# Three attentions of a two-layer block: scores ahead of values, side work behind the next step's maxima

## The chip, the cores and the metric

One core of a Trainium2 chip runs the whole kernel. The metric is the device time of one execution in microseconds (us); before the change the median of three runs is 1392.32 us (1392.32 to 1393.35).

## The reference, cut to what matters

256 tokens of width 1024 pass through two blocks. The first has an attention and a gated mixer, then a mixture of 16 experts (each 1024 to 2048 to 1024, top choices by capacity). The second has a layer with two attentions (causal, and sliding window with sinks), then a layer with a causal attention whose scores carry a cumulative forget gate. The core of all attentions is the same:

```python
s = jnp.einsum('bqhd,bkhd->bhqk', qi, k) * scale      # + bias, gate or window
s = jnp.where(mask, s, -jnp.inf)
p = jax.nn.softmax(s, axis=-1)
out = jnp.einsum('bhqk,bkhd->bqhd', p.astype(v.dtype), v)
...
return x + (o * jax.nn.silu(gate)) @ w_out
```

## The kernel before, in words

Each engine has its own program, written out by hand, and they meet in semaphores: `pe_program`, `dve_program`, `act_program`, `pool_program`, `sp_program`. An engine works strictly in the order of its program. TensorE (PE) multiplies, VectorE (DVE) and ScalarE (ACT) work on SBUF and PSUM, GpSimd (POOL) does a few small things and subtractions, SP issues the loads.

Weights come through a ring of seven slots of 2 MB. SP goes through the list of loads in order (L754 to L757); before each it waits until the slot's former content has been used. Three loads go to places lent by other tiles; two of them wait for the last values of the first attention (L290). Where accuracy wants it a weight is split in two: ACT rounds a quarter of it (`hi_piece`, L448, its instruction L454), then DVE or POOL subtracts (`lo_piece`, L456, L460).

PSUM has eight banks. `banks.take` deals six of them (`ALL6`) in turn; whoever takes one waits until its former content is out. Two banks are kept for the attentions' outputs.

An attention is a row of steps, each with two halves (g or r = 0, 1) of 512 scores per token. A step n has this chain:
- scores: PE (first attention L898; second L1136, L1139; third L1212, L1214);
- maxima: DVE (L1450, L1451; `largest`, L596 to L607, which also copies the scores to SBUF);
- exponents: ACT (L1936; `exponents`, L615, L618);
- division: DVE (L1460, L1462; `divide`, L625 to L630);
- transposes: PE (L479);
- copy of the transposed probabilities to SBUF: half 0 on ACT, half 1 on DVE (`probabilities_out`, `turned_out`; instructions L510 and L508);
- values: PE (L915, for two steps at a time; `values_flipped`, L582).

The first attention has 8 steps (`A1`), the second and third have 6 each (`A2`, `A3`), first one with 128 keys, two and two with 256, one with 128.

In iteration n PE does scores n, a turn, transposes n-1, a turn, values n-1. DVE does the end of a gate (`gate_finish`), maxima n, a turn, the gated product of an output that ended, copy n-1, division n, a turn, the gated low part. ACT does exponents n, copy n-1, the gated high part, and two turns (in the first attention one turn stands before the copy).

A turn runs one piece of side work from a generator. In the first attention (`beside`) that is, on PE: modulation products `mod_part` (L777), the spatial mixing (L839), columns (`mod_cols`, L789) and parts of the out-projection (L502); on DVE and ACT: its mixtures, weight splits and modulation rows. In the second and third attention it is the gate's projection: PE does it in quarters (`gate_matmuls`, L681); after each fourth quarter DVE multiplies (L716), ACT takes tanh (L699), and DVE finishes with `gate_finish` (L729) in the next iteration. ACT also splits weights (`gate_act`): the first four pieces go to POOL, the rest to DVE after the attention. When an output has ended, `gated` makes the product (DVE, L655), the high part (ACT, L663) and the low part (DVE, L659), which waits for the high part. Then come the out-projections (L502 second, L490 third attention).

```python
    def turn(side):
        next(side, None)
```

Of the kernel before, what the change touches and what calls it, by code (L numbers as in the profile page):

```python
# [139 lines left out]
def body(ctx, nc, A, kin, out):  # L140
# [620 lines left out]
    def pe_program(pe):  # L761
# [100 lines left out]
        def beside():  # L862
# [21 lines left out]
            for n2 in (1, 2):  # L884
                out_part(n2, True)
                yield

        side = beside()
        for n in range(9):
            if n < 8:  # L890
                i, hn = A1[n]
                for g in range(2):
                    banks.take((1, "s", n, g), ALL6)
                for g in range(2):
                    pe.wait_ge(banks.was[1, "s", n, g])
                pe.wait_ge(out_of(("QT", 0)), out_of(("QT", 1)), out_of("KT"))
                for g in range(2):
                    pe.e.matmul(PS[:, banks.of[1, "s", n, g], :], QT[64 * g:64 * g + 64, i, 128 * hn:128 * hn + 128],  # L898
                                KT[64 * g:64 * g + 64, :], start=True, stop=True).then_inc(*pe.mark((1, "s", n, g)))
            turn(side)  # L900
            if n:
                for g in range(2):
                    pe.wait_ge((1, "p", n - 1, g))
                    transposes(pe, (1, "t", n - 1, g), ALL6,
                               [PB[(2 * (n - 1) + g) % 4][:, 128 * s:128 * s + 128] for s in range(4)])
            turn(side)
            if n and n % 2 == 0:
                batch, i = n // 2 - 1, (n - 1) // 4
                if batch % 2 == 0:
                    banks.take((1, "o", i), (OB[i],))  # L910
                    pe.wait_ge(banks.was[1, "o", i])
                pe.wait_ge(out_of(("kv", 3)), *[out_of((1, "t", m_, g)) for m_ in (n - 2, n - 1) for g in range(2)])
                for s in range(4):
                    for g in range(2):
                        m = pe.e.matmul(PS[64 * g:64 * g + 64, OB[i], 256 * (batch % 2):256 * (batch % 2) + 256],  # L915
                                        KV[:, s, 128 + 64 * g:192 + 64 * g], PTB[batch % 2][:, s, g, :], start=s == 0,
                                        stop=s == 3)
                m.then_inc(*pe.mark((1, "pv", batch), *([(1, "o", i)] if batch % 2 else [])))
        rest(side)

# [200 lines left out]
        for n in range(len(A2) + 1):  # L1121
            if n < len(A2):
# [9 lines left out]
                for hh in range(len(step["heads"][0])):  # L1132
                    for r in range(2):
# [7 lines left out]
                        score_mark(pe, m, "e", n, r, hh == len(step["heads"][0]) - 1)  # L1141
            turn(side)
            if n:
                for r in range(2):
                    pe.wait_ge(("e", "p", n - 1, r))
                    transposes(pe, ("e", "t", n - 1, r), ALL6,
                               [A2_PB[(2 * (n - 1) + r) % 4][:, 128 * s:128 * s + 128] for s in range(4)])
            turn(side)
            if n:
# [4 lines left out]
                else:  # L1154
                    pe.wait_ge(out_of(("kvup", 1, 1)))
                    values_flipped(pe, "e", A2[n - 1], n - 1, A2_PT, 2, lambda s, h: VM[:, s, h, :])
        rest(side)

# [42 lines left out]
        pe.wait_ge(*[out_of((nm, n2)) for nm in ("q0", "q1", "k0", "k1") for n2 in range(2)], out_of("flT"), "kq")  # L1201
        for n in range(len(A3) + 1):
            if n < len(A3):
# [5 lines left out]
                for hh in range(len(step["heads"][0])):  # L1209
                    for r in range(2):  # L1210
# [5 lines left out]
                        score_mark(pe, m, "o", n, r, hh == len(step["heads"][0]) - 1)  # L1216
            turn(side)
            if n:
                for r in range(2):
                    pe.wait_ge(("o", "p", n - 1, r))  # L1220
                    transposes(pe, ("o", "t", n - 1, r), ALL6,
                               [A3_PB[(2 * (n - 1) + r) % 4][:, 128 * s:128 * s + 128] for s in range(4)])
            turn(side)
            if n:
                pe.wait_ge(*[out_of(("vf", h, i)) for h in range(2) for i in range(2)])
                values_flipped(pe, "o", A3[n - 1], n - 1, A3_PT, 2, lambda s, h: VF[:, s, 64 * h:64 * h + 64])
        rest(side)
        for i in (1, 0):
# [23 lines left out]
    def dve_program(dve):  # L1252
# [188 lines left out]

        side = beside()
        for n in range(9):
            if n < 8:
                i, hn = A1[n]
                for g in range(2):
                    idx = 8 * i + 4 * g + hn
                    c = slice(idx, idx + 1)
                    dve.wait_ge((1, "s", n, g))
                    dve.settle(dve.e.tensor_reduce(mx1[:, c], PS[:, banks.of[1, "s", n, g], :], AX.X, ALU.max))  # L1450
                    dve.e.tensor_scalar(nm1[:, c], mx1[:, c], -0.125, None, ALU.mult).then_inc(*dve.mark((1, "nm", n, g)))  # L1451
            turn(side)
            if n:
                probabilities_out(dve, n - 1, 1)
            if n < 8:
                for g in range(2):
                    idx = 8 * i + 4 * g + hn
# [3 lines left out]
                    p = PB[(2 * n + g) % 4]  # L1461
                    dve.e.tensor_scalar(p, p, sm1[:, c], None, ALU.mult).then_inc(*dve.mark((1, "p", n, g)))  # L1462
            turn(side)
            if n == 5:
# [196 lines left out]
        dve.wait_ge(*[out_of((name, hp)) for name in ("QMT", "KMT") for hp in range(4)], "bias")  # L1661
        for n in range(len(A2) + 1):
            gate_finish(dve, "e", late)
            if n < len(A2):
                step, nk = A2[n], A2[n]["nk"]
                for r in range(2):
# [7 lines left out]
            turn(side)  # L1674
            ended = A2[n - 2] if n >= 2 and A2[n - 2]["last"] else None
            if ended:
                gated(dve, None, "e", ended, OT, ("product",))
            if n:
                turned_out(dve, "e", n - 1, 1, A2_PT, 2)
            if n < len(A2):  # L1680
                for r in range(2):
                    divide(dve, "e", A2[n], n, r, A2_PB[(2 * n + r) % 4], sm2 if A2[n]["part"] == "mla" else sm3,
                           columns(A2[n], r, 8), sinks=A2[n]["part"] == "swa")
            turn(side)
            if ended:
# [93 lines left out]
        dve.wait_ge(out_of("cumulated"))  # L1779
        for n in range(len(A3) + 1):  # L1780
            gate_finish(dve, "o", late)
# [6 lines left out]
            turn(side)  # L1788
            ended = A3[n - 2] if n >= 2 and A3[n - 2]["last"] else None
            if ended:  # L1790
                gated(dve, None, "o", ended, OT3, ("product",))
            if n:
                turned_out(dve, "o", n - 1, 1, A3_PT, 2)
            if n < len(A3):
                for r in range(2):
                    divide(dve, "o", A3[n], n, r, A3_PB[(2 * n + r) % 4], sm4, columns(A3[n], r, 16))
            turn(side)
            if ended:
# [45 lines left out]
    def act_program(act):  # L1844
# [83 lines left out]
        act.wait_ge(out_of(("QT", 0)), out_of(("QT", 1)), out_of("KT"), "kr")  # L1928
        for n in range(9):
            if n < 8:  # L1930
                i, hn = A1[n]
                for g in range(2):
# [5 lines left out]
                        *act.mark((1, "e", n, g), out_of((1, "s", n, g))))  # L1938
            turn(side)
            if n:  # L1940
                probabilities_out(act, n - 1, 0)
            turn(side)
            if n == 5:
# [115 lines left out]
        for n in range(len(A2) + 1):  # L2059
            if n < len(A2):  # L2060
                swa = A2[n]["part"] == "swa"
                for r in range(2):
                    exponents(act, "e", A2[n], n, r, A2_PB[(2 * n + r) % 4], nm3 if swa else nm2, sm3 if swa else sm2,
                              columns(A2[n], r, 8), sinks=swa)
            if n:
                turned_out(act, "e", n - 1, 0, A2_PT, 2)
            if n >= 2 and A2[n - 2]["last"]:
                gated(None, act, "e", A2[n - 2], OT, ("high",))
# [36 lines left out]
        for _ in range(4):  # L2105
            turn(side)
        for n in range(len(A3) + 1):
            if n < len(A3):
                for r in range(2):
                    exponents(act, "o", A3[n], n, r, A3_PB[(2 * n + r) % 4], nm4, sm4, columns(A3[n], r, 16))  # L2110
            if n:
                turned_out(act, "o", n - 1, 0, A3_PT, 2)
            if n >= 2 and A3[n - 2]["last"]:
                gated(None, act, "o", A3[n - 2], OT3, ("high",))
# [201 lines left out]
```

## Time and profile before

| | us |
|---|---|
| median of three runs | 1392.32 |
| the profiled execution's own time | 1392.85 |
| its span | 1391.1 |
| TensorE busy | 993.2 |
| VectorE busy | 408.8 |
| ScalarE busy | 239.8 |
| GpSimd busy | 81.8 |
| share of DMA in the chain that ended last | 57% |
| share of TensorE in that chain | 32% |

The span is what the profile covers; the execution's own time has 1.75 us more around it. Busy times are sums over the span and say nothing of what lies beside what. "Idle before" with a releaser is the time that an engine stood idle before an instruction, and whose end released it. Times within the span are counted from its start.

### The profile page before, as it was taken

The page shows a single profiled execution, that of the slowest core. Times are in us where ns is not written, and L with a number is a line of the kernel's source. Part 1 is how long each engine was busy: PE and PEld are TensorE (multiplying, and loading weights), DVE is VectorE, ACT ScalarE, POOL GpSimd, SP SyncE. Part 2 cuts the span into 40 slices and gives each one's busy share as a digit, 9 for nine tenths or more (in the row PEclk, how much of TensorE's full clock was granted, in tenths as well). Part 3 has the DMA queues.
Part 4 walks back from the last instruction along what each step waited for, and adds up shares of the span by engine and source line. Part 5 has one row for each costly group of instructions (what it writes and reads, how often), then busy time and mean ns, then how long its engine had stood idle before and what let it go on. Part 6 is the DMA issues. An engine that isn't in the chain of part 4 may idle for free.

```text
span 1391.1 us, 15218 instructions
## 1 busy us (share of the span) xinstructions
PE 993.2 (71%) x6623; PEld 511.7 (37%) x6623; DVE 408.8 (29%) x966; ACT 239.8 (17%) x483; POOL 81.8 (6%) x74
## 2 busy tenths in 40 slices
PE   4998987666675665756656566656556789899987
PEld 3865842212121111111111111111111588799875
DVE  4756421011011100101011010110101467785584
ACT  3534210000000000000000000000000355543452
POOL 1300000000020000000000000000000053200020
PEclk9999899789787888788788877887877798999998
DMA  9996789999999999999999999999999451144311
GB/s 399 380 371 235 325 354 429 427 428 427 428 426 428 429 428 428 425 429 428 428 428 427 427 428 428 427 428 429 425 428 429 183 220 62 61 182 175 133 57 46
DMA packets 34771, 482.47 MB, mean 347 GB/s; under 512 B 3854, under 2 KB 3856, under 8 KB 5520
## 3 DMA queue, kind: packets, MB, share of 16 engines
q1 hardware_dynamic: 34240, 479.92, 82.4%
q8 instruction: 52, 0.85, 0.2%
q10 hardware_dynamic: 288, 1.05, 0.2%
q0 software_dynamic: 176, 0.53, 0.1%
q14 instruction: 15, 0.12, 0.0%
HBM read 480.43 MB, written 1.05 MB: 346 GB/s over the span
## 4 chain that ended last, share of the span: by engine, by line
DMA 57%; PE 32%; DVE 5%; ACT 3%; issue 1%; POOL 1%; SPq 0%; POOLq 0%; DVEq 0%; ACTq 0%
DMA ring<-in_t_w 53%; PE PS L502 7%; PE PS L490 6%; PE PS L1000 5%; PE PS L1046 3%; DMA ring<-in_t_e_a 2%; DMA ring<-in_t_mod 2%; ACT S L615 2%; PE PS L681 1%; PE PS L479 1%; PE PS L799 1%; PE PS L777 1%; PE PS L582 1%; POOL RR L460 1%; DVE S L596 1%
## 5 line engine op out<-in xcount | busy, mean ns | idle before, releaser
L1000 PE MATMUL PS<-ring,S 128*32 128x512 f32 x2016 | 317.0, 761 | 216.8 <-DMA ring<-in_t_w 214.3
L1046 PE MATMUL PS<-ring,S 128*32 128x512 f32 x1008 | 171.8, 816 | 103.3 <-DMA ring<-in_t_w 94.4
L1000 PEld LDWEIGHTS PS<-ring,S 128*32 128x32 f32 x2016 | 61.9, 125 | 449.6 <-DMA ring<-in_t_w 334.4
L508 DVE COPY S<-PS 128x512 f32<-128x512 f32 (+2 forms) x47 | 32.1, 683 | 310.3 <-PE PS L1046 291.3
L502 PE MATMUL PS<-SR,RR 128*128 128x256 f32 x736 | 117.4, 285 | 1.2 <-DVE ab L1432 0.9
L1046 PEld LDWEIGHTS PS<-ring,S 128*32 128x32 f32 x1008 | 33.7, 131 | 224.3 <-DMA ring<-in_t_w 147.5
L502 PEld LDWEIGHTS PS<-SR,RR 128*128 128x128 f32 x736 | 103.7, 189 | 2.5 <-DVE ab L1432 1.2
L454 ACT ACTIVATE RR<-ring 128x1024 fp32r<-128x1024 f32 (+3 forms) x95 | 89.5, 1005 | 38.4 <-DMA ring<-in_t_e_a 18.0
L1548 DVE TENSOR_SCALAR S<-PS,KC 128x256 f32<-128x256 f32 x16 | 7.7, 484 | 280.4 <-PE PS L1030 280.4
L510 ACT ACTIVATE S<-PS 128x512 f32<-128x512 f32 (+2 forms) x50 | 27.9, 568 | 343.1 <-PE PS L479 338.2
L460 DVE TENSOR_TENSOR RR<-ring,RR 128x1024 fp32r<-128x1024 f32 (+2 forms) x76 | 84.2, 1155 | 8.5 <-ACT RR L454 8.5
L1995 ACT ACTIVATE S<-PS 128x512 f32<-128x512 f32 x16 | 9.6, 597 | 438.4 <-PE PS L1000 438.4
L490 PE MATMUL PS<-RR,SR 128*128 128x512 f32 (+3 forms) x264 | 76.1, 399 | 0.0
L1558 DVE TENSOR_TENSOR S<-PS,S 128x512 f32<-128x512 f32 x16 | 11.1, 692 | 209.3 <-PE PS L1000 209.3
L479 PE MATMUL PS<-KC,S 128*128 128x128 f32 (+1 forms) x308 | 46.0, 295 | 27.7 <-DVE S L1263 14.7
L502 PE MATMUL PS<-RR,RR 128*128 128x256 f32 x224 | 62.9, 281 | 0.0
L1538 DVE SCALAR_TENSOR_TENSOR X<-PS,ab,X 128x256 f32<-128x256 f32 x128 | 51.9, 476 | 18.9 <-PE PS L1013 18.9
L479 PEld LDWEIGHTS PS<-KC,S 128*128 128x128 f32 (+1 forms) x308 | 36.9, 150 | 55.4 <-DVE S L1558 35.9
L681 PE MATMUL PS<-SR,RR 128*128 128x256 f32 x256 | 52.4, 304 | 4.1 <-POOL RR L460 3.5
L490 PEld LDWEIGHTS PS<-RR,SR 128*128 128x128 f32 x264 | 50.5, 194 | 11.1 <-issue 0.3
L460 POOL TENSOR_TENSOR RR<-ring,RR 128x1024 fp32r<-128x1024 f32 (+1 forms) x19 | 44.6, 2374 | 133.6 <-ACT RR L454 133.6
L681 PEld LDWEIGHTS PS<-SR,RR 128*128 128x128 f32 x256 | 42.0, 201 | 7.2 <-POOL RR L460 4.1
(311 smaller groups left out, 962.2 us busy)
## 6 DMA issues: line engine op xcount, KB each, us to landing
ring<-in_t_w SPq DMA_DIRECT2D x189, 2048.0 KB, 31.3
ring<-in_t_mod SPq DMA_DIRECT2D x12, 2048.0 KB, 13.0
ring<-in_t_out SPq DMA_DIRECT2D x6, 2048.0 KB, 8.0
S<-in_t_w SPq DMA_DIRECT2D x3, 2048.0 KB, 12.1
ring<-in_t_e_g SPq DMA_DIRECT2D x2, 2048.0 KB, 7.8
ring<-in_t_o_q SPq DMA_DIRECT2D x2, 2048.0 KB, 8.0
ring<-in_t_o_k SPq DMA_DIRECT2D x2, 2048.0 KB, 8.8
ring<-in_t_o_v SPq DMA_DIRECT2D x2, 2048.0 KB, 8.4
```

The source lines that it names most:

```text
L454: act.e.activation(hi[:, c:c + step, :], dst[:, c:c + step, :], ACT.Copy).then_inc(*act.mark(("hi", key, c)))
L460: lane.e.tensor_tensor(lo[:, c:c + step, :], place[key][:, c:c + step, :], hi[:, c:c + step, :].bitcast(F32), ALU.subtract).then_inc(*lane ...
L479: t = pe.e.transpose(PS[0:parts, b, 128 * i:128 * i + 128], in_, ident)
L490: m = pe.e.matmul(PS[:, b, 0:width], l_, r_, start=(k == ks[0] and n == 0), stop=(k == ks[-1] and n == 2))
L502: m = pe.e.matmul(PS[:, b, 256 * nn:256 * nn + 256], l_, r_, start=(k == ks[0] and m_ == 0), stop=(k == ks[-1] and m_ == 2))
L508: lane.e.tensor_copy(dst, src).then_inc(*lane.mark(out_of(key), *names))
L510: lane.e.activation(dst, src, ACT.Copy).then_inc(*lane.mark(out_of(key), *names))
L615: t = act.e.activation(p[:, c], p[:, c], ACT.Exp, bias=nm[:, i_:i_ + 1], accum_out=sm[:, i_:i_ + 1])
L681: m = pe.e.matmul(PS[:, b, 256 * nn:256 * nn + 256], l_, r_, start=(k == 0 and m_ == 0), stop=(k == 7 and m_ == 2))
L1000: m = pe.e.matmul(PS[32 * j:32 * j + 32, b, :], expert_rows(2 * k + kk, e_, e_ + 1), place[name, e_, k][:, kk, 512 * j:512 * j + 512], sta ...
L1046: m = pe.e.matmul(PS[q:q + 32, b, :], HT[e_ % 2][:, 128 * s + 32 * j:128 * s + 32 * j + 32], place["w2", e_, j][:, s, 512 * dh:512 * dh + ...
L1538: t = dve.e.scalar_tensor_tensor(out=XT[:, k, :], in0=PS[:, banks.of[key], o:o + 256], scalar=ab[:, 7, k:k + 1], in1=XT[:, k, :], op0=ALU. ...
```

## The change

All three attentions are rewritten in the same manner. The scores, maxima and exponents become functions, are called once for step 0 ahead of the loop, and in iteration n for step n+1:
- PE: transposes n-1, scores n+1, turn, values n-1, turn. (In the first attention iteration 0 has both turns behind the scores of step 1.)
- DVE: `gate_finish`, copy n-1, division n, maxima n+1, turn, gated product, turn, gated low part.
- ACT: copy n-1, exponents n+1, gated high part, turn, turn.

The first attention cut to its core, and the second on DVE:

```diff
         side = beside()
+        scores(0)
         for n in range(9):
-            if n < 8:
-                i, hn = A1[n]
...
-            turn(side)
             if n:
                 for g in range(2):
                     pe.wait_ge((1, "p", n - 1, g))
                     transposes(pe, (1, "t", n - 1, g), ALL6,
                                [PB[(2 * (n - 1) + g) % 4][:, 128 * s:128 * s + 128] for s in range(4)])
+            if n + 1 < 8:
+                scores(n + 1)
             turn(side)
+            if n == 0:
+                turn(side)
             if n and n % 2 == 0:
...
                 m.then_inc(*pe.mark((1, "pv", batch), *([(1, "o", i)] if batch % 2 else [])))
+            if n:
+                turn(side)
         rest(side)
...
+        largest_even(0)
+        for n in range(len(A2) + 1):
+            gate_finish(dve, "e", late)
             if n:
                 turned_out(dve, "e", n - 1, 1, A2_PT, 2)
             if n < len(A2):
                 for r in range(2):
                     divide(dve, "e", A2[n], n, r, A2_PB[(2 * n + r) % 4], sm2 if A2[n]["part"] == "mla" else sm3,
                            columns(A2[n], r, 8), sinks=A2[n]["part"] == "swa")
+            largest_even(n + 1)
+            turn(side)
+            ended = A2[n - 2] if n >= 2 and A2[n - 2]["last"] else None
+            if ended:
+                gated(dve, None, "e", ended, OT, ("product",))
             turn(side)
             if ended:
                 gated(dve, None, "e", ended, OT, ("low",))
...
+        exponents_even(0)
+        for n in range(len(A2) + 1):
             if n:
                 turned_out(act, "e", n - 1, 0, A2_PT, 2)
+            exponents_even(n + 1)
             if n >= 2 and A2[n - 2]["last"]:
                 gated(None, act, "e", A2[n - 2], OT, ("high",))
             turn(side)
```

## Rows read from the trace of the kernel before

**Rows 1.** Stretches: us, then busy us (count) of each engine, TensorE's granted clock, DMA.
```profile
250.00:1060.00 810.00, 500.63 (x3041) 128.18 (x3033) 84.11 (x198) 21.10 (x41) 8.14 (x13) 0.81 1.01 428
...
1157.00:1212.00 55.00, 46.27 (x393) 41.89 (x392) 46.35 (x164) 34.63 (x97) 12.18 (x7) 0.97 0.21 77
```

**Rows 2.** SP's issues in order of time: start, length, line, tile, count.
```profile
186.43 143.81 SPq L756 DMA_DIRECT2D ring<-in_t_w  x35
```

**Rows 3.** The chain that ended last: start, us, what.
```profile
1060.77 29.62 DMA ring<-in_t_e_a
...
1211.78 16.80 PE PS L502 x138
...
1359.13 1.19 PE PS L582 x16
```

**Rows 4.** TensorE's waits, 84 to 147 us: total, times, longest.
```profile
PE PS L915 <- ACT S L510: 4.7, 2, 2.6
PE PS L915 <- DVE st L1460: 1.5, 1, 1.5
PE PS L502 <- DVE ab L1432: 0.9, 1, 0.9
PE PS L789 <- ACT bm L510: 0.8, 2, 0.6
```

**Rows 5.** First attention in order of time: start, length, instructions, idle before.
```profile
97.46 1.95 PE L915 MATMUL PS<-S 128*64 128x256 f32 x16 [1.45 <-DVE st L1460]
...
99.34 1.13 PE L898 MATMUL PS<-S 64*128 64x512 f32 x4
...
109.93 2.95 PE L915 MATMUL PS<-S 128*64 128x256 f32 x16 [2.65 <-ACT S L510]
...
112.81 1.77 PE L898 MATMUL PS<-S 64*128 64x512 f32 x4
...
114.61 0.69 DVE L1450 TENSOR_REDUCE st<-PS 128x1 f32<-128x512 f32 x1 [4.01 <-PE PS L898]
```

**Rows 6.** VectorE's waits, 1157 to 1204 us, and last 1311 to 1360 us.
```profile
DVE S L596 <- PE PS L1139: 2.5, 3, 1.4
DVE SG L729 <- ACT PS L699: 2.0, 3, 0.7
DVE st L625 <- ACT st L618: 0.5, 2, 0.4
...
DVE S L596 <- PE PS L1214: 3.5, 2, 2.6
```

**Rows 7.** Second attention in order of time, GpSimd and VectorE.
```profile
1184.41 4.71 POOL L460 TENSOR_TENSOR RR<-ring,RR 128x1024 fp32r<-128x1024 f32 x2 [2.66 <-ACT RR L454]
...
1186.87 2.28 DVE L607 TENSOR_SCALAR st<-st 128x2 f32<-128x2 f32 x1
...
1195.65 0.17 DVE L607 TENSOR_SCALAR st<-st 128x4 f32<-128x4 f32 x1
...
1196.69 0.17 DVE L607 TENSOR_SCALAR st<-st 128x4 f32<-128x4 f32 x1
```

**Rows 8.** VectorE's groups by shape, 1157 to 1204 us: busy, mean ns, idle before.
```profile
L630 DVE TENSOR_SCALAR S<-S,st 128x256 f32<-128x256 f32 x16 | 4.9, 350 | 0.3
L607 DVE TENSOR_SCALAR st<-st 128x2 f32<-128x2 f32 x4 | 4.7, 1187 | 0.1
...
L630 DVE TENSOR_SCALAR S<-S,st 128x128 f32<-128x128 f32 x16 | 3.5, 282 | 0.1
```

**Rows 9.** ScalarE in the second attention: chain (first two), then order of time.
```profile
1189.18 2.08 ACT S L615 x8
...
1195.86 3.20 ACT S L615 x16
...
1183.29 1.04 ACT L454 ACTIVATE RR<-ring 128x1024 fp32r<-128x1024 f32 x1
...
1191.64 0.62 ACT L663 ACTIVATE SR<-bm 128x512 fp32r<-128x512 f32 x1
```

More of the change, by code:

```diff
@@ L886, in beside, with scores @@
                 yield
+        def scores(n):
+            i, hn = A1[n]
+            for g in range(2):
+                banks.take((1, "s", n, g), ALL6)
+            for g in range(2):
+                pe.wait_ge(banks.was[1, "s", n, g])
+            pe.wait_ge(out_of(("QT", 0)), out_of(("QT", 1)), out_of("KT"))
+            for g in range(2):
+                pe.e.matmul(PS[:, banks.of[1, "s", n, g], :], QT[64 * g:64 * g + 64, i, 128 * hn:128 * hn + 128],
+                            KT[64 * g:64 * g + 64, :], start=True, stop=True).then_inc(*pe.mark((1, "s", n, g)))
         side = beside()
+        scores(0)
         for n in range(9):
-            if n < 8:
-                i, hn = A1[n]
[L892 to L899, printed above, removed]
-            turn(side)
             if n:
@@ L1120, in pe_program, with scores_even @@
                 transposes(pe, (name, hp), ALL6, [src[:, i, 2 * hp + hh, :] for hh in range(2) for i in range(2)], parts=96)
-        for n in range(len(A2) + 1):
+        def scores_even(n):
             if n < len(A2):
@@ L1141, in pe_program @@
                         score_mark(pe, m, "e", n, r, hh == len(step["heads"][0]) - 1)
-            turn(side)
+        scores_even(0)
+        for n in range(len(A2) + 1):
             if n:
@@ L1147, in pe_program @@
                                [A2_PB[(2 * (n - 1) + r) % 4][:, 128 * s:128 * s + 128] for s in range(4)])
+            scores_even(n + 1)
             turn(side)
@@ L1201, in pe_program, with scores_odd @@
         pe.wait_ge(*[out_of((nm, n2)) for nm in ("q0", "q1", "k0", "k1") for n2 in range(2)], out_of("flT"), "kq")
-        for n in range(len(A3) + 1):
+        def scores_odd(n):
             if n < len(A3):
@@ L1216, in pe_program @@
                         score_mark(pe, m, "o", n, r, hh == len(step["heads"][0]) - 1)
-            turn(side)
+        scores_odd(0)
+        for n in range(len(A3) + 1):
             if n:
@@ L1222, in pe_program @@
                                [A3_PB[(2 * (n - 1) + r) % 4][:, 128 * s:128 * s + 128] for s in range(4)])
+            scores_odd(n + 1)
             turn(side)
@@ L1226, in pe_program @@
                 values_flipped(pe, "o", A3[n - 1], n - 1, A3_PT, 2, lambda s, h: VF[:, s, 64 * h:64 * h + 64])
+            turn(side)
         rest(side)
@@ L1442, in dve_program, with maxima @@
         side = beside()
-        for n in range(9):
[L1444 to L1452, printed above, removed]
+        def maxima(n):
+            i, hn = A1[n]
+            for g in range(2):
+                idx = 8 * i + 4 * g + hn
+                c = slice(idx, idx + 1)
+                dve.wait_ge((1, "s", n, g))
+                dve.settle(dve.e.tensor_reduce(mx1[:, c], PS[:, banks.of[1, "s", n, g], :], AX.X, ALU.max))
+                dve.e.tensor_scalar(nm1[:, c], mx1[:, c], -0.125, None, ALU.mult).then_inc(*dve.mark((1, "nm", n, g)))
+        maxima(0)
+        for n in range(9):
             if n:
@@ L1455, in dve_program @@
             if n < 8:
+                i, hn = A1[n]
                 for g in range(2):
@@ L1462, in dve_program @@
                     dve.e.tensor_scalar(p, p, sm1[:, c], None, ALU.mult).then_inc(*dve.mark((1, "p", n, g)))
+            if n + 1 < 8:
+                maxima(n + 1)
+            turn(side)
             turn(side)
@@ L1661, in dve_program, with largest_even @@
         dve.wait_ge(*[out_of((name, hp)) for name in ("QMT", "KMT") for hp in range(4)], "bias")
-        for n in range(len(A2) + 1):
-            gate_finish(dve, "e", late)
+        def largest_even(n):
             if n < len(A2):
@@ L1673, in dve_program @@
                                 0.125, lower=sinkb[:, hs[0]:hs[-1] + 1:2])
[L1674 to L1677, printed above, removed]
+        largest_even(0)
+        for n in range(len(A2) + 1):
+            gate_finish(dve, "e", late)
             if n:
@@ L1683, in dve_program @@
                            columns(A2[n], r, 8), sinks=A2[n]["part"] == "swa")
+            largest_even(n + 1)
+            turn(side)
+            ended = A2[n - 2] if n >= 2 and A2[n - 2]["last"] else None
+            if ended:
+                gated(dve, None, "e", ended, OT, ("product",))
             turn(side)
@@ L1779, in dve_program, with largest_odd @@
         dve.wait_ge(out_of("cumulated"))
-        for n in range(len(A3) + 1):
-            gate_finish(dve, "o", late)
+        def largest_odd(n):
             if n < len(A3):
@@ L1787, in dve_program @@
                             lambda h: cmask[:, 256 - nk:256], 0.125, shift=fl[:, step["i"], hs[0]:hs[-1] + 1:2])
[L1788 to L1791, printed above, removed]
+        largest_odd(0)
+        for n in range(len(A3) + 1):
+            gate_finish(dve, "o", late)
             if n:
@@ L1796, in dve_program @@
                     divide(dve, "o", A3[n], n, r, A3_PB[(2 * n + r) % 4], sm4, columns(A3[n], r, 16))
+            largest_odd(n + 1)
+            turn(side)
+            ended = A3[n - 2] if n >= 2 and A3[n - 2]["last"] else None
+            if ended:
+                gated(dve, None, "o", ended, OT3, ("product",))
             turn(side)
@@ L1928, in act_program, with exponents_mix @@
         act.wait_ge(out_of(("QT", 0)), out_of(("QT", 1)), out_of("KT"), "kr")
-        for n in range(9):
+        def exponents_mix(n):
             if n < 8:
@@ L1938, in act_program @@
                         *act.mark((1, "e", n, g), out_of((1, "s", n, g))))
-            turn(side)
+        exponents_mix(0)
+        for n in range(9):
             if n:
                 probabilities_out(act, n - 1, 0)
+            exponents_mix(n + 1)
+            turn(side)
             turn(side)
@@ L2058, in act_program, with exponents_even @@
                          PS[0:96, banks.of[name, hp], :].rearrange("p (h t) -> p h t", h=2))
-        for n in range(len(A2) + 1):
+        def exponents_even(n):
             if n < len(A2):
@@ L2064, in act_program @@
                               columns(A2[n], r, 8), sinks=swa)
+        exponents_even(0)
+        for n in range(len(A2) + 1):
             if n:
                 turned_out(act, "e", n - 1, 0, A2_PT, 2)
+            exponents_even(n + 1)
             if n >= 2 and A2[n - 2]["last"]:
@@ L2106, in act_program, with exponents_odd @@
             turn(side)
-        for n in range(len(A3) + 1):
+        def exponents_odd(n):
             if n < len(A3):
@@ L2110, in act_program @@
                     exponents(act, "o", A3[n], n, r, A3_PB[(2 * n + r) % 4], nm4, sm4, columns(A3[n], r, 16))
+        exponents_odd(0)
+        for n in range(len(A3) + 1):
             if n:
                 turned_out(act, "o", n - 1, 0, A3_PT, 2)
+            exponents_odd(n + 1)
             if n >= 2 and A3[n - 2]["last"]:
```

## The prediction

> **What bounds the kernel now.** I read the busy time by stretch first. From 250 to 1060 us the DMA engines are full (share 1.01, 428 GB/s), while TensorE is busy 501 of 810 us [rows 1]: the expert weights set the pace there. The issues of SP show where that stream begins: 35 loads in unbroken succession from 186.43 us, each waiting for a ring slot that the experts' first matmuls give back [rows 2]. The chain of waits says the same from the other end: the last link of the stream is the load that lands at 1090.4 [rows 3]. So the middle is a block of fixed length. What happens in the first attention (84 to 145 us) moves its start, and the second and third attention (1157 to 1207, 1311 to 1360) lie behind it on a path of computing. All three count in full, each by what moves its own exit.
>
> In the first attention TensorE is the engine that has to get through: it idles only 7.9 us (4.7 + 1.5 + 0.9 + 0.8) [rows 4]. The largest case is instructive: the values at 109.93 wait 2.65 us for ACT's copy; the next scores stand behind them (112.81, 1.77 us instead of 1.13 at 99.34, the values 2.95 instead of 1.95 at 97.46), and DVE stood idle 4.01 us for these scores [rows 5]. In the second attention VectorE is the engine: 46.35 of 55 us busy [rows 1]. It waits 2.5 us for scores and 2.0 us for tanh [rows 6], and part of its busy time is a stall: the small TENSOR_SCALAR takes 2.28 us at 1186.87 and 0.17 at 1195.65, and the long one ends when GpSimd's two subtractions (1184.41 to 1189.12) end [rows 7].
>
> **What the change does.** Written out for DVE, before: maxima n, copy n-1, division n. After: copy n-1, division n, maxima n+1. Laid end to end this is the same order. ACT too keeps its order of exponents and copies. What moves is (1) on PE, the scores n+1 ahead of the values n-1; (2) on all engines, the side work: on DVE both turns, the gated product and low part, and the end of a gate (L729) now stand between maxima n+1 and copy n; on ACT everything stands behind the exponents of n+1, no longer those of n; (3) on PE the second turn comes behind the values. No instruction and no DMA is added or removed. SP's program is untouched, but its slots are freed elsewhere.
>
> **First attention.** I walked the three queues with the times of before. PE does S0, S1 (1.13), two modulation products, T0, S2, and so on. Maxima 2 begin at 92.2, maxima 3 at 95.9, maxima 4 at 102.3, maxima 5 at 107.8 against 114.61 before: the scores no longer stand behind the stalled values. Then ACT's weight copies, put behind the exponents of the next step, become late: TensorE waits 1.35 us for division 5, 1.85 for the modulation row, 0.95 for copy 5 and 0.7 for the last row. Sum 4.85 in place of 7.9, and I give back the 1.64 us by which the slow pair ran over (2.95 - 1.95, 1.77 - 1.13) [rows 5]: 7.9 - 4.85 + 1.64 = **4.7 us earlier** at the end of the out-projection's first half, the experts and the stream. If a slow stretch of that size comes again it is 3.0; if each new wait is double, nothing; if all 7.9 and 1.6 go, 9.5. I take 4.7, since the one long wait that I can see is cut at its cause. The moved modulation products release ring slots at most 1.1 us later at the start, where DMA is full anyway, and 3 us sooner at the end; the two loads at 145.3, tied to the last values, would go at 138. They are preloads and give nothing by themselves.
>
> **Second attention.** Here DVE has the list. Gone: 2.5 us for scores and 0.5 for the exponents of step 0 (L625's waits, filled with L729) [rows 6]. New, each read from what ACT has ahead of the thing waited for. The exponents of a pair take 2.08 us at 256 keys and 3.20 at 128 [rows 9].
> - End of a gate behind step 2: the second exponents run on 1.1 us after the maxima, tanh 0.6 more (2.0 in three waits [rows 6]), L716 covers 0.6: wait 1.2. Behind step 4 a weight copy of 1.04 [rows 9] comes between: 2.1. The last: 0.7 as before. Together 4.0 against 2.0.
> - Low part (L659), which follows ACT's high part (0.62) [rows 9]. At step 3: 1.1 + 0.6 - 0.6 for the product = 1.1. At 128 keys the maxima of a half take 1.04 (1195.65 to 1196.69) [rows 7] and the exponents 3.20, so they run on 2.15 after the maxima: wait 2.1. Step 6: 0.7. At the end the high part stands behind two weight copies: 1.4 against 0.7 + 0.5. Together 5.3 against 1.2.
> - GpSimd. Its four subtractions (2.36 each) follow ACT's weight copies, which now come right ahead of a copy and a division. DVE leaves its wait, copies (0.6 like any pass over 512 elements, L663's for one) and reaches the first 128x256 product of the division 1.9 us before the first subtraction ends; then the second subtraction takes its turn, and the second product waits 2.35 more: 4.25. With the second pair the tanh lies between: 0.35 + 2.35 = 2.7. Together 6.95. Before: four small L607 of 1.187 us in place of 0.17 [rows 7, 8], 4.1.
>
> Sum: -2.5 - 0.5 + 2.0 + 4.1 + 2.85 = +5.95 us. From this 1.5 comes off: laid on a time line, step by step, the same walk ends at 1211.1 instead of 1206.8, as a wait that I list singly is partly used up by the neighbour before it. I take **+4.4 us**. DVE's subtractions for the out-projection and PE at 1211.78 [rows 3] follow directly. Bounds: no stall at all in the divisions is 4.4 - 6.95 = -2.5; the four subtractions each stalling in full (9.4) is +6.9. Nearest is the measured pattern [rows 7]: an instruction that meets a subtraction waits to its end.
>
> No row of before shows a 128x256 TENSOR_SCALAR meeting GpSimd; if it ran beside it, the second attention would be the lower bound. What speaks for it: its time grows from 282 to 350 ns for 128 more elements [rows 8], half a nanosecond each, as a doubled rate would. The Trainium skill ("SBUF — State Buffer", Who interferes with whom) says that VectorE in a two-port mode, which tensor_scalar can enter, or with two SBUF inputs, takes an exclusive lock with GpSimd, and the second one blocks fully. By that rule the sum is as above, and the trace agrees with it (2.28 us for 0.17).
>
> **Third attention.** Same walk; its steps have the same sizes. Gone are 3.5 us of waits for scores [rows 6]; the new waits and stalls are those above. VectorE finishes the last division 2.0 us later. But the exit is not its end: the values of the last step go at 1359.13 [rows 3], behind L716, tanh, L729, product and copy of before (3.4 us after the division); now the product comes later, so only 2.6 lie between. 2.0 - 0.8 = **+1.1 us** with rounding. The low parts and DVE's subtractions are needed by later matmuls of the 24 us projection and stay hidden (their cover is the first 24 matmuls). Bounds: -1.5 (no stalls in divisions, cover full) and +3.5.
>
> **Sum.** -4.7 + 4.4 + 1.1 = +0.8 us. The profiled execution took 1392.85 (span 1391.1), 0.53 above the median of 1392.32; the difference applies to the median: 1393.1. A measurement of this kernel can tell about 0.2%, 2.8 us, from no change.
>
> **Rivals.**
> 1. *The pipeline pays.* TensorE's early scores save 4.7 to 6 at the front, and the division misses GpSimd (the weight copies fall beside waits). Second -1, third -1: about 1386. For it: 2.5 and 3.5 us of waits for scores vanish surely. Against: the low part waits behind the exponents by order of the queue. Chance 0.13. A weaker form, with the front at -6 and the rest as forecast or half of it, gives 1388 to 1389.5; chance 0.07.
> 2. *The division's products run beside GpSimd unhindered*, and only small instructions such as L607 stall. Then -2.5 and -1.5 with -4.7: 1383.6. Against: L607 is the same operation in fewer elements. Chance 0.03.
> 3. *Waits behind ACT eat the front too* (slower). Mechanism: ACT's modulation row and weight copies in the first attention stand behind exponents whose maxima come late; TensorE waits at cols a, values 2 and cols g, and each long wait can be followed by slower matmuls, as the pair after the 2.65 us wait (1.64 us longer [rows 5]). If TensorE's waits there reach 7.5 us instead of 4.85 the front gains only 2.0, and the time is 1395.8; from 6.8 us on it is slower by more than 0.2%. Chance 0.14.
> 4. *Every subtraction stalls VectorE in full*: the second attention at +6.9 and the third at +1.6, 1396.1. Against: DVE's copy and L729 come from PSUM and run meanwhile. Chance 0.11.
> 5. *The change does nothing*: VectorE's and ACT's order is the same as before, and only covers move. The time stays at 1392; it lies within my forecast's side. For it: the order as written out above.
>
> Forecast, within 0.2%: 0.52 (of it 0.1 for rival 5). Faster by over 0.2% (below 1389.5): 0.23. Slower (above 1395.1): 0.25. The range leaves out the strongest forms of 1 and 2 and the sum of 3 and 4: 1387.5 to 1397.
>
> **What would show it.** In the first attention: PE's wait before the values of step 4 gone, no 4 us wait of DVE for scores, experts' first matmul at 178.5 and the last stream load landing at 1085.7. In the second: no DVE wait for scores; L659 waiting for ACT 1 and 2 us; L729 waiting 1 to 2 us; L630 at 2 to 2.4 us several times, L607 at 0.17. Length from the first maxima to the last low part 54 us instead of 49.9. If the loads' stream does not start earlier, the front is wrong; if L630 is never long, the second attention is.

## The result, and the profile after

| | before | changed |
|---|---|---|
| median, us (17 runs each) | 1392.24 | 1395.68 |
| range, us | 1389.85 to 1395.04 | 1393.04 to 1400.32 |
| profiled execution, us | 1392.85 | 1394.48 |
| its span, us | 1391.1 | 1392.7 |

The ratio is 1.0033, 95% interval 1.0025 to 1.0042: slower by 4.6 us (3.5 to 5.8). The medians are 3.4 us apart. The profiled execution of the changed kernel is the fifth fastest of its 17, so its stretches are compared, and its total isn't.

**The front.** The issues of SP, and the chain of waits with the last link of the stream:

```profile
180.31 143.92 SPq L756 DMA_DIRECT2D ring<-in_t_w  x35
```
```profile
1054.15 30.18 DMA ring<-in_t_e_a
```

The experts' stream starts 6.1 us sooner than before [rows 2] and its last link 6.6 sooner [rows 3]; 1.5 of it is there ahead of the first attention. (That 1.5 us is chance: in 3 of the 10 profiled executions with the changed first attention its first maxima start at 82.8 or 82.9 us, in the other 7 at 84.2 to 84.6, as in the 4 with the old one.) TensorE's waits from 84 to 147 us, beside 7.9 us before [rows 4]:

```profile
PE PS L789 <- ACT bm L510: 3.0, 2, 2.2
PE PS L920 <- DVE st L1477: 0.9, 1, 0.9
PE PS L479 <- DVE S L1479: 0.8, 1, 0.8
```

The first attention in order of time (L896 are the scores, L920 the values, L1464 the maxima; L898, L915 and L1450 before [rows 5]):

```profile
104.73 1.95 PE L920 MATMUL PS<-S 128*64 128x256 f32 x16
107.63 1.13 PE L896 MATMUL PS<-S 64*128 64x512 f32 x4
...
112.63 1.13 PE L896 MATMUL PS<-S 64*128 64x512 f32 x4
...
117.92 3.35 PE L920 MATMUL PS<-S 128*64 128x256 f32 x16 [0.93 <-DVE st L1477]
```

and the first maxima of step 5:

```profile
105.52 0.68 DVE L1464 TENSOR_REDUCE st<-PS 128x1 f32<-128x512 f32 x1
```

The values of a pair of steps (104.73) have no wait in front of them, the scores take 1.13 us, and the maxima of step 5 start at 105.5, with no wait, where they started at 114.61 after 4 us of waiting [rows 5]. One set of values (117.92) still runs at 3.35 us.

**The second attention.** VectorE's groups, 1151 to 1208 us (busy, mean ns, idle before):

```profile
L630 DVE TENSOR_SCALAR S<-S,st 128x128 f32<-128x128 f32 (+1 forms) x32 | 14.7, 512 | 0.4
...
L659 DVE SCALAR_TENSOR_TENSOR RR<-bm,SR 128x512 fp32r<-128x512 f32 x4 | 2.8, 692 | 5.0 <-ACT SR L663 5.0
L729 DVE SCALAR_TENSOR_TENSOR SG<-PS,SG 128x512 f32<-128x512 f32 x4 | 2.8, 689 | 3.7 <-ACT PS L699 3.7
...
L716 DVE TENSOR_TENSOR SG<-PS,cvec 128x512 f32<-128x512 f32 x3 | 2.1, 686 | 3.0 <-PE PS L681 3.0
...
L607 DVE TENSOR_SCALAR st<-st 128x2 f32<-128x2 f32 (+1 forms) x6 | 1.0, 169 | 0.2
```

The division's products (L630) cost 14.7 us for the same 32 instructions, 4.9 + 3.5 before, and L607 is at 0.17 us again, 4.7 for four before [rows 8]. Where the long products come from, in order of time:

```profile
1174.05 4.75 POOL L460 TENSOR_TENSOR RR<-ring,RR 128x1024 fp32r<-128x1024 f32 x2 [24.57 <-ACT RR L454]
1183.70 4.74 POOL L460 TENSOR_TENSOR RR<-ring,RR 128x1024 fp32r<-128x1024 f32 x2 [4.90 <-ACT RR L454]
```
```profile
1174.46 4.49 DVE L630 TENSOR_SCALAR S<-S,st 128x256 f32<-128x256 f32 x2
1179.06 0.61 DVE L630 TENSOR_SCALAR S<-S,st 128x256 f32<-128x256 f32 x2
...
1184.14 0.69 DVE L729 SCALAR_TENSOR_TENSOR SG<-PS,SG 128x512 f32<-128x512 f32 x1 [2.10 <-ACT PS L699]
1184.75 0.68 DVE L508 COPY S<-PS 128x512 f32<-128x512 f32 x1
1185.53 3.05 DVE L630 TENSOR_SCALAR S<-S,st 128x256 f32<-128x256 f32 x2
```

The pair that meets GpSimd's subtractions takes 4.49 and 3.05 us, the next pair 0.61. In both cases it ends 0.15 us after GpSimd's second subtraction (1178.95 and 1178.80, 1188.58 and 1188.44). The end of the attention, from the chain of waits:

```profile
1190.39 3.19 ACT S L615 x16
1194.13 0.69 DVE RR L659
1195.57 1.98 PE PS L582 x16
1197.55 2.87 PE PS L681 x12
1200.44 0.70 DVE SG L716
```

This is what the prediction does not have. VectorE waits for ACT's high part, so its copy comes late, so TensorE idles 4.1 us and starts the values late. The last gate quarter (L681) stands behind these values, and VectorE waits 3.0 us for it. TensorE's granted clock has fallen by then; the windows, with the clock in the third column from the end:

```profile
1151.00:1190.00 39.00, 32.81 (x276) 28.42 (x273) 33.23 (x128) 19.99 (x66) 9.48 (x4) 1.00 0.15 55
1190.00:1208.00 18.00, 11.93 (x83) 10.88 (x82) 10.29 (x33) 9.58 (x26) 0.24 (x1) 0.72 0.32 117
```

Much of the 3.0 us is this clock. At a granted clock of 1.00 the 16 values take 1.09 us, here 1.98; and three gate matmuls start every 0.35 us (1190.22, 1190.57, 1190.92), which makes 12 of them an estimated 1.4 us, here 2.87. Together that is about 2.3 us, an estimate too.

**Stretches of all kernels.** One measure serves for every run below: from the start of the first L596 (maxima) of an attention to the start of its last L659 (low part), and from there to the end of the span.

| profiled execution | second, us | third, us | last low part to end, us |
|---|---|---|---|
| before | 48.6 | 49.3 | 29.3 |
| changed | 55.6 | 53.3 | 26.8 |
| first only | 48.6 | 49.3 | 29.2 |
| second only | 55.1 | 49.5 | 29.1 |
| third only | 48.6 | 53.4 | 26.8 |
| changed, no GpSimd | 49.6 | 49.4 | 26.9 |
| scores early only | 47.3 | 47.3 | 27.9 |
| the same, finish behind maxima | 50.6 | 48.1 | 28.6 |
| changed, turns before values | 52.5 | 51.4 | 26.8 |
| the same, no GpSimd | 47.1 | 46.3 | 26.8 |
| before, no GpSimd | 48.4 | 47.2 | 28.8 |
| scores early, no GpSimd (first, second launch) | 48.8, 50.7 | 49.7, 49.7 | 29.0, 29.0 |
| first only, no GpSimd | 48.4 | 47.2 | 28.8 |

In the third attention L630 is long in the same manner (4.52 and 3.05 us in the chain), and in its last iteration VectorE waits for a gate quarter too, where before the last division's products ran straight into L716:

```profile
1359.48 0.69 DVE L716 TENSOR_TENSOR SG<-PS,cvec 128x512 f32<-128x512 f32 x1 [1.78 <-PE PS L681]
```

Behind it the projection begins with TensorE at a higher clock: 0.96 from 1360 to 1370 us, 0.83 before. Its 96 matmuls took 24.03 us before; in the changed kernel:

```profile
1363.37 22.60 PE PS L490 x96
```

### The profile page after: what moved, and what is told of

The parts are those of the page before. It is cut to its first block, busy times and chain, and to the rows that moved or that the text cites. A ratio compares the mean times of both kernels' runs of the same rounds, so it can differ in the third digit from the quotient of the medians.

```text
span 1392.7 us, 15218 instructions
## 1 busy us (share of the span) xinstructions
PE 993.1 (71%) x6623; PEld 513.2 (37%) x6623; DVE 411.6 (30%) x966; ACT 239.1 (17%) x483; POOL 81.3 (6%) x74
## 4 chain that ended last, share of the span: by engine, by line
DMA 57%; PE 30%; DVE 7%; ACT 3%; issue 1%; POOL 1%; SPq 0%; POOLq 0%; DVEq 0%; ACTq 0%
DMA ring<-in_t_w 53%; PE PS L502 8%; PE PS L490 5%; PE PS L1007 5%; PE PS L1053 3%; DMA ring<-in_t_e_a 2%; DVE S L630 2%; DMA ring<-in_t_mod 2%; ACT S L615 2%; PE PS L681 1%; PE PS L479 1%; PE PS L777 1%; DVE S L596 1%; DVE S L508 1%; PE PS L799 1%
## 5 line engine op out<-in xcount | busy, mean ns | idle before, releaser
L502 PE MATMUL PS<-SR,RR 128*128 128x256 f32 x736 | 118.2, 286 | 0.0
L502 PEld LDWEIGHTS PS<-SR,RR 128*128 128x128 f32 x736 | 104.6, 190 | 1.0 <-issue 0.7
L460 DVE TENSOR_TENSOR RR<-ring,RR 128x1024 fp32r<-128x1024 f32 (+2 forms) x76 | 84.2, 1155 | 13.1 <-ACT RR L454 13.1
L510 ACT ACTIVATE S<-PS 128x512 f32<-128x512 f32 (+2 forms) x50 | 27.9, 568 | 341.9 <-PE PS L479 337.0
L479 PE MATMUL PS<-KC,S 128*128 128x128 f32 (+1 forms) x308 | 49.2, 305 | 33.5 <-DVE S L1278 14.7
L502 PE MATMUL PS<-RR,RR 128*128 128x256 f32 x224 | 63.3, 283 | 0.0
L681 PE MATMUL PS<-SR,RR 128*128 128x256 f32 x256 | 54.5, 312 | 3.5 <-POOL RR L460 3.5
L490 PEld LDWEIGHTS PS<-RR,SR 128*128 128x128 f32 x264 | 49.8, 191 | 10.8 <-issue 0.2
L681 PEld LDWEIGHTS PS<-SR,RR 128*128 128x128 f32 x256 | 43.6, 209 | 7.8 <-POOL RR L460 4.1
```

Of the source, the lines that this page charges most:

```text
L460: lane.e.tensor_tensor(lo[:, c:c + step, :], place[key][:, c:c + step, :], hi[:, c:c + step, :].bitcast(F32), ALU.subtract).then_inc(*lane ...
L479: t = pe.e.transpose(PS[0:parts, b, 128 * i:128 * i + 128], in_, ident)
L490: m = pe.e.matmul(PS[:, b, 0:width], l_, r_, start=(k == ks[0] and n == 0), stop=(k == ks[-1] and n == 2))
L502: m = pe.e.matmul(PS[:, b, 256 * nn:256 * nn + 256], l_, r_, start=(k == ks[0] and m_ == 0), stop=(k == ks[-1] and m_ == 2))
L510: lane.e.activation(dst, src, ACT.Copy).then_inc(*lane.mark(out_of(key), *names))
L681: m = pe.e.matmul(PS[:, b, 256 * nn:256 * nn + 256], l_, r_, start=(k == 0 and m_ == 0), stop=(k == 7 and m_ == 2))
```

## The experiments

The kernel before had medians of 1391.26, 1392.21, 1391.39 and 1392.24 us in the four launches, each on another chip. Differences below are the ratio's, against before in the same launch, with its 95% interval; each run below has 6 to 12 executions. Where two changed kernels are set against each other, the error follows from both intervals and is an estimate.

### One attention at a time

Each takes the change in the functions of one attention alone, on all three engines. The core of the edit on TensorE, here for the second:

```diff
-            turn(side)
...
+            scores_even(n + 1)
             turn(side)
             if n:
...
                     values_flipped(pe, "e", A2[n - 1], n - 1, ...)
+            turn(side)
```

> Only the first attention is rewritten. Theory A (the traces: the start of the long load stream came 6.1 us sooner, 1.5 of it already there when the attention began): 4.6 us faster than before, about 1387.6. Theory B (the front is not what the end waits for; the stream of loads swallows it): no change, 1392.

> Only the second attention is rewritten. Theory A (the traces: a lead of 6.0 us at its entry became a lag of 0.6 at its exit): 6.6 us slower, about 1398.8. As forecast: 4.4 us slower, 1396.6. Theory B (most of it was this execution's luck): under 2 us slower.

> Only the third attention is rewritten. Theory A (the traces: exit 2.4 us later, then the projection's first matmuls run 1.4 us faster since TensorE did not stand as long before them): 1.0 us slower, about 1393.2. Theory B (nothing comes back in the projection): 2.4 us slower, 1394.6. The three changes alone should add up to the whole: +3 to +4.

Measured: first only 1386.08, **-5.4 us** (-7.7 to -3.3). Second only 1396.93, **+5.0** (+3.3 to +6.7). Third only 1394.26, **+2.5** (+0.4 to +4.5). The sum is +2.1 where the whole measured +4.6; with errors of about 2 us on each part this is no contradiction. So the change is a gain at the front and two losses behind it. The interval of second only rules out its theory B, under 2 us; it holds the forecast's 4.4 and just so theory A's 6.6. The third attention's holds both of its theories, +1.0 and +2.4, and decides nothing between them.

### GpSimd's subtractions given to VectorE

```diff
+            if n == 3:
+                lo_piece(dve, ("out2", 0), 0)
+                lo_piece(dve, ("out2", 0), 2)
             turn(side)
...
-        lo_all(pool, ("out2", 0))
```

Two more pieces follow in iteration 4, and the third attention has the same with out3. VectorE has more work by this edit, GpSimd less.

> The changed kernel, but the four subtractions per attention that GpSimd did beside the second and third attention are done by VectorE, two after the maxima of step 4 and two before the low part of step 4's iteration, where it waits for ScalarE. Theory A (the divisions stall on GpSimd: L630 4.49 and 3.05 us where 0.61 is usual, in both attentions): 6.3 us less per attention, 4.9 us of work more, of which about 4 fall into waits: 5 to 6 us less each, 1384 to 1386. Theory B (the waits for ScalarE set the length, the stalls only fill them): no gain or slower, 1395 to 1400.

> The kernel before, with the subtractions that GpSimd does in the second and third attention given to VectorE, as in the changed kernel without them. Theory A (GpSimd held VectorE up in one 2.28 us reciprocal step of the second attention already before the change, and in little else, and VectorE pays about 1.3 us an attention for the work): within 2 us of before, -2 to +1, so that most of the 11.7 us the same edit took off the changed kernel was made by the change. Rival B (the edit helps any order of the work by the same): -8 to -11.

Measured: on the changed kernel 1385.15, **-7.1** (-9.9 to -4.5), so 11.7 us less than the changed kernel (about 3 either way). On the kernel before 1388.83, **-2.6** (-3.9 to -1.4), a little more than its theory A allowed and far from B. (The 2.28 us step that its text calls a reciprocal is L607, the small TENSOR_SCALAR.) VectorE's group of the second attention on the changed kernel without GpSimd, beside 14.7 us above:

```profile
L630 DVE TENSOR_SCALAR S<-S,st 128x128 f32<-128x128 f32 (+1 forms) x32 | 8.4, 316 | 0.4
```

The same edit is worth 2.6 us in the old order and 11.7 in the new one: 9.1 us of its worth (about 3 either way) were made by the change. These are net sums, as VectorE has four subtractions more per attention, 1.22 us each. The traces agree: the two attentions and the end are 2.8 us shorter by the edit in the old order and 9.9 in the new one. In the old order that is 0.2 us in the second attention and 2.1 in the third. Without GpSimd the change as a whole is a gain, -7.1 against -2.6, so the collision decides the sign. The gain is still the first attention's: in the second and third together with the end, the changed order without GpSimd is 1.5 us longer than the old order without it.

### The turns of the gate ahead of the values

```diff
             scores_even(n + 1)
             turn(side)
+            turn(side)
             if n:
                 values_flipped(pe, "e", A2[n - 1], n - 1, ...)
-            turn(side)
```

> The changed kernel, with both turns of the gate ahead of the values on TensorE in the second and third attention. Theory A (3.0 us of the second attention and part of the third's 3.0 are VectorE's wait for gate quarters that stand behind the values): -3 to -4 against the changed kernel, +0.5 to +1.5 against before, 1392. Rival B (those waits only show earlier what the last low part's wait would show, or the values are late by the same): as the changed kernel, +4.6, 1396.

> The same, and the subtractions that GpSimd does beside the division are done by VectorE. Theory A (the two costs are separate and add): -10 to -11 against before, 1381. Rival B (the wait for gate quarters, which grew to 6.6 us in the second attention when GpSimd's work went to VectorE, was cover and not cost): no better than the kernel without GpSimd's subtractions alone, -7, 1385.

Measured: 1392.19, **+1.2** (-0.1 to +2.6), so 3.4 us less than the changed kernel (about 2 either way). With GpSimd's work on VectorE too 1381.81, **-10.8** (-13.9 to -7.7), the best of all. VectorE's waits, 1154.5 to 1209 us, in the kernel with the turns moved alone:

```profile
DVE RR L659 <- ACT SR L663: 5.0, 4, 2.1
DVE SG L729 <- ACT PS L699: 3.7, 3, 2.1
DVE S L596 <- PE PS L1143: 0.5, 1, 0.5
```

L716's wait of 3.0 us is gone, every other row is as in the changed kernel, and the second attention is 3.1 us shorter (55.6 to 52.5), the third 1.9. Theory A is right in both: the wait was a cost of its own, and it adds to the collision. With both mended the changed order pays in the second and third attention as well: 4.2 us shorter with the end than the old order without GpSimd.

### VectorE and ScalarE in the old order, scores early on TensorE

Here the second and third attention have the loops of before on VectorE and ScalarE. On TensorE the next scores and both turns stand ahead of the values.

> First attention as in the changed kernel; in the second and third VectorE and ScalarE keep the order of before, and only TensorE is changed: turns, the next step's scores, values. Theory A (the pipelining of TensorE is worth its waits; what costs is that side work now stands in the division): first attention -5 as it measured alone, second and third lose their 2.5 and 3.0 us waits for scores, so about -9 to -10 against before, 1382. Rival B (the waits for scores only hide the GpSimd collision and ScalarE's exponents, so nothing beyond the first attention's gain is had): -5 to -6, 1386. Both expect no 4 to 5 us in L630 in the trace if the division stays where it was.

Measured: 1386.04, **-7.8** (-10.7 to -4.9). It lies between the two theories. The division no longer meets GpSimd (longest L630 0.35 us), but the small L607 does (median 0.91 us), and VectorE waits 1.4 us for a gate quarter. The traces give 1.3 and 2.1 us for the second and third attention and 1.3 for the end, against first only; the ratios 2.4 us in all, less than their errors.

```diff
-            gate_finish(dve, "e", late)
             if n < len(A2):
                 ... maxima ...
+            gate_finish(dve, "e", late)
             turn(side)
```

> The same, and the end of the gate half (gate_finish) is moved on VectorE from ahead of the next maxima to behind them, so that ScalarE's part of it is ready. Theory A: the 2.0 us wait of L729 and its counterpart in the third attention go, another -2 to -4 against the kernel with early scores alone, some 1379. Rival: the finish lands in front of the copy of the weights and its wait moves to the next one, no change (within 1 us).

Measured: 1388.25, **-5.0** (-7.1 to -2.9). A miss for both: no gain, and 2.2 us worse in the median, though the two intervals overlap. In the trace the second attention is 3.3 us longer. L729's wait did go there (2.0 to 0.7), but the wait for gate quarters grew from 1.4 to 5.9 us. The division met GpSimd again (L630 12.7 us instead of 8.4), while L607 no longer did (1.0 instead of 5.4). In the third attention a low part met GpSimd and took 2.85 us instead of 0.69.

### The remaining combinations

> VectorE and ScalarE of before in the second and third attention, scores early on TensorE, first attention as changed, and no subtractions on GpSimd. Theory A (in the order of before GpSimd costs little; early scores keep their gain): -8 to -11. Rival B (even without GpSimd the changed order of VectorE is the better one, because the next exponents start earlier): above -8, so slower than the changed kernel with both mendings, which measured -10.4.

> Only the first attention changed, and no subtractions on GpSimd: what the second and third bring when scores are neither early nor GpSimd in the way. Theory A (sum of the parts): -5.4 -2 to +1, so -4 to -8, and 2 to 4 us slower than with early scores. Rival B (waits for scores cover nothing and cost nothing): as with early scores.

Measured: early scores without GpSimd 1392.06, **+0.4** (-0.7 to +1.7): far from theory A, and on B's side. First only without GpSimd 1385.04, **-6.3** (-8.6 to -4.0), as theory A has it from the parts; but A also held it to be 2 to 4 us slower than with early scores, and it is 6.7 us faster. Against that kernel the mended second and third attention are worth another 4.5 us (about 4 either way), and 4.2 us in the traces.

The first of these was unexplained, so it was run again.

> The same kernel as the one with early scores and no GpSimd, once more, since its 12 runs stood 5 us above its own profiled execution and 6 us above the same kernel with GpSimd. Theory A (the kernel is slower: VectorE's wait for gate quarters and a slower granted clock of TensorE in the third attention, 2.4 us in its trace, and more of the same in most executions): again 1391 to 1393, within 0.1% of before, and a profiled execution near it shows the length of the second and third attention above 48.5 and 49.7 us. Rival B (the chip or the moment: the granted clock in stretches that no edit touches): -6 to -9 against before, as the sum of parts would have it.

Measured: 1392.01, **-1.8** (-3.9 to +0.4). No gain of 6 to 9 us again: it repeats. In both profiled executions the third attention takes 49.7 us where the kernel with GpSimd takes 47.3. Windows at its end, the second launch:

```profile
1340.00:1350.00 10.00, 9.51 (x96) 8.88 (x96) 9.82 (x29) 3.29 (x10) 0.00 (x0) 1.00 0.01 2
1350.00:1360.00 10.00, 4.98 (x35) 4.28 (x37) 7.38 (x28) 7.07 (x22) 0.00 (x0) 0.65 0.00 0
```

and the kernel that leaves the subtractions on GpSimd:

```profile
1350.00:1360.00 10.00, 7.98 (x61) 6.53 (x62) 7.94 (x14) 6.17 (x9) 0.68 (x1) 1.00 0.04 14
```

VectorE's own subtractions now stand ahead of the division (2.27 us a pair, in the chain). TensorE is busy 5 of 10 us, and its granted clock is 0.65 in the stretch; 16 values take 1.98 us instead of 1.09, and the 96 matmuls of the projection 23.71 instead of 22.61. That is one place and 3.5 us of it (49.7 - 47.3 and 23.71 - 22.61); the second attention has another 1.5 us in the first launch and 3.4 in the second. Why the same four subtractions help the changed order and hurt this one was argued from the chain and not tested by itself.

## Why the prediction was right or wrong

The time forecast was 1393.1; the median is 1395.68, inside the range. The likeliest case, no change, did not come; the one with a chance of 0.25 did. That the time lies inside the range is in part luck, as the three attentions show.

- **The block of fixed length.** Right. The last link of the stream was issued at 1060.2 us on average in the four profiled executions whose first attention was as before, and at 1055.6 in the ten others: 4.6 us sooner, of which 0.5 is the earlier entry that three of the ten had.
- **The first attention, -4.7.** Right in size, and in its waits, but not in every term: -5.4 as a kernel, 4.6 by the links. The maxima of step 5 start at 105.5, 107.0 with the 1.5 us of an earlier entry put back; 107.8 was forecast. TensorE waits 4.7 us where 4.85 was forecast, and in the four places that were named: the modulation row 2.2 (forecast 1.85), the last row 0.8 (0.7), the copy of step 5 0.9 (0.95), its division 0.8 (1.35). The stretch of slow values came back (3.35 for 1.95), at another step than before; for that case the forecast had 3.0 us. Counted from the attention's first maxima, the 35 loads start 4.6 us sooner in this execution and 2.9 on average of the ten. What makes up the rest of the kernel's -5.4 is not shown. Rival 3, waits behind ACT eating the front, did not happen.
- **The second attention, +4.4.** This is the step that failed: +7.0 in length, and its end goes from 6.0 us ahead at the first scores to 0.6 behind at the exit, so +6.6. As a kernel +5.0. Term by term, forecast and measured: scores -2.5, -2.3; exponents -0.5, -0.5; end of a gate +2.0, +1.5; low part +4.1, +4.3; GpSimd +2.85, +2.2 (L630 +6.3, L607 -4.1); other small waits 0, -1.0; gate quarter 0, **+3.0**. Without the gate quarter the measured terms sum to +4.2, beside the +4.4 that was taken. So the list was nearly right, and so was some deduction from it: 1.0 of the 1.5 us taken off are the small waits that went. What was missing is one term. Part (3) of the description, the second turn behind the values, was named and never priced: in the last iteration no maxima stand ahead to cover it, and TensorE comes to it late and at a lower clock.
- **"No row of before shows a 128x256 TENSOR_SCALAR meeting GpSimd."** Now rows do: 4.49 and 3.05 us for a pair that takes 0.61, so 3.9 and 2.4 us of stall where 4.25 and 2.7 were forecast. The mechanism was forecast, and without the collision the change does not lose (-7.1). Rival 2 fell. Rival 4 gave the nearest time (1396.1) for the wrong reason: the subtractions stalled VectorE 6.3 us of the 9.4 it supposes, and the rest was the gate quarter.
- **The rule of the Trainium skill.** The copy from PSUM at 1184.75 and L729 at 1184.14 run at their usual 0.68 us while GpSimd subtracts, and the products with SBUF at both ends stall. The small reciprocals (L626, 0.15 us), which have SBUF at both ends too, do not. The Trainium skill ("SBUF — State Buffer", Who interferes with whom) says that an instruction in a two-port mode and GpSimd exclude each other for whole instructions, and the trace agrees with it.
- **The third attention, +1.1.** Right in size in the trace, by luck: +4.0 in length, then -2.5 to the end and -0.5 ahead of it, so +1.0. As a kernel +2.5 (+0.4 to +4.5). The last division ends 2.0 us later, counted from the first maxima, as forecast. But from there to the last values it takes 4.6 us where 2.6 was forecast and 3.5 was before: the gate quarter again, 1.8 us. What makes up for it, 24.03 to 22.60 us in the projection, the forecast did not have.
- **The chances.** With the gate quarter of the second attention the forecast's sum is +0.8 + 3.0 = +3.8, beside +4.6 measured. Rival 1, the pipeline pays, needed the division to miss GpSimd; the kernels in which it does measured -7.1 and, with the turns moved, -10.8, of which -2.6 is had in the old order too.

## What to carry to other kernels

When a software pipeline is deepened, list for every engine what now stands between a producer and its consumer in the last iteration too, where the work that covered it has run out. Look where the second engine on a shared memory port runs: moving the same four subtractions of each attention off that engine was worth 2.6 us in one order and 11.7 in another, and lost 6 to 8 in a third; with the gate's turns ahead of the values it turned +4.6 us into -10.8. A wait that is removed in one place is worth only what the next one in the chain leaves.

## What the runs showed of the hardware

The stretch between the stream and the second attention, which no edit touches, differs by up to 8.5 us between profiled executions: from the issue of the stream's last link to the first maxima of the second attention 96.8 us before, 91.9 with the first attention only and no GpSimd, 100.4 in the changed kernel without GpSimd. The windows of the kernel with the first attention only and no GpSimd, then of the changed kernel without GpSimd:

```profile
1100.00:1110.00 10.00, 10.00 (x70) 9.95 (x70) 5.05 (x13) 3.84 (x10) 4.52 (x5) 1.00 0.21 65
```
```profile
1100.00:1110.00 10.00, 10.00 (x38) 9.72 (x38) 3.36 (x8) 1.80 (x2) 2.45 (x3) 0.50 0.00 0
```

TensorE is busy throughout in both and does 70 matmuls in one and 38 in the other: 2.4 GHz (granted clock 1.00) against 1.2 GHz (0.50). In both, the L1070 matmuls behind the stream start at 1092.9 us, and TensorE had been busy alike (5.8 of 8 us from 1084 to 1092, 7.1 of 8 from 1092 to 1100); the L502 matmuls behind them start at 1106.8 us in the one and at 1113.2 in the other, so 6.4 us are this clock. What decides which clock is granted the traces do not show. Single executions of these kernels lie 5 to 13 us apart, and this is one source of it. So the total of one execution is a poor witness for an edit of 3 us, while the length of an attention is a better one, though it differs too (50.7 and 48.8 us for one kernel in two launches).
